# Twelve spare slots for the next expert's weights in a mixture-of-experts loop, emptied into the ring by GpSimd copies

## The reference, cut to what matters

```python
def moe_ffn(h, w_router, b_router, w_gate, b_gate, w_up, b_up, w_down, b_down):
    ...
    top_vals, top_idx = lax.top_k(logits, TOP_K)
    top_gates = jax.nn.softmax(top_vals, axis=-1)
    ...
    def expert_block(args):
        xb, e = args
        gate = xb @ w_gate[e] + b_gate[e]
        up = xb @ w_up[e] + b_up[e]
        gate = jnp.minimum(gate, SWIGLU_LIMIT)
        up = jnp.clip(up, -SWIGLU_LIMIT, SWIGLU_LIMIT)
        glu = gate * jax.nn.sigmoid(SWIGLU_ALPHA * gate)
        return (glu * (up + 1.0)) @ w_down[e] + b_down[e]
```

## Time and profile before

| | us |
|---|---|
| median of 3 runs | 2936.56 |
| lowest and highest run | 2932.51, 2937.8 |
| the profiled execution, its own time | 2935.62 |
| its span, first to last instruction | 2933.9 |
| TensorE busy in the span | 2772.3 |
| VectorE busy | 1529.7 |
| ScalarE busy | 956.0 |
| GpSimd busy | 116.1 |

### The profile page before, as it was taken

The page is one execution under the profiler, slowest core; times in us unless marked ns, Lnnn a source line. Parts: engine busy times, 40 slices in busy tenths (PEclk is TensorE's granted clock), DMA queues, the critical chain, the costliest instruction groups (busy, mean ns, idle before and its releaser), DMA issues.

```text
span 2933.9 us, 38779 instructions
## 1 busy us (share of the span) xinstructions
PE 2772.3 (94%) x12664; PEld 1659.5 (57%) x12664; DVE 1529.7 (52%) x3078; ACT 956.0 (33%) x1805; POOL 116.1 (4%) x171
## 2 busy tenths in 40 slices
PE   7899999999999999999999989999998999998997
PEld 5676678888778667888877753332322332322332
DVE  5984778875673554334385544343333343332435
ACT  4734342222563434222333322322222232222231
POOL 0000000000000003000020000000000000000002
PEclk9999999999999999999999979999999999999999
DMA  8271246864323035342323079689899789899897
GB/s 268 72 215 42 89 130 185 238 185 130 94 86 86 15 86 171 95 119 79 97 73 106 1 279 409 267 349 410 319 410 409 297 322 410 319 410 410 326 407 285
DMA packets 398912, 638.18 MB, mean 218 GB/s; under 512 B 34576, under 2 KB 284560, under 8 KB 398816
## 3 DMA queue, kind: packets, MB, share of 16 engines
q1 hardware_dynamic: 381024, 590.80, 55.9%
q0 software_dynamic: 9376, 31.14, 3.1%
q10 hardware_dynamic: 8416, 14.95, 1.4%
HBM read 610.79 MB, written 26.02 MB: 217 GB/s over the span
## 4 chain that ended last, share of the span: by engine, by line
PE 73%; DMA 9%; SPq 5%; DVE 5%; ACT 4%; issue 2%; POOL 0%; ACTq 0%; DVEq 0%; POOLq 0%
PE bank L2620 24%; PE bank L196 14%; PE bank L198 14%; PE bank L197 13%; DMA ring<-w_down 6%; SPq L2430 4%; DMA ring<-w_gate 2%; PE bank L1084 1%; PE bank L1125 1%; PE bank L1085 1%; DVE WLO L167 1%; ACT WHI L157 1%; PE bank L2614 1%; PE bank L1118 0%; ACT la L411 0%
## 5 line engine op out<-in xcount | busy, mean ns | idle before, releaser
L2620 PE MATMUL bank<-ring,xT 128*64 128x512 f32 x3200 | 728.8, 597 | 24.6 <-DMA ring<-w_up 12.7
L196 PE MATMUL bank<-HH,WHI 128*128 128x512 f32 x1344 | 540.2, 402 | 34.5 <-DVE WLO L167 17.3
L197 PE MATMUL bank<-HL,WHI 128*128 128x512 f32 x1344 | 529.9, 394 | 0.0
L198 PE MATMUL bank<-HH,WLO 128*128 128x512 f32 x1344 | 529.6, 394 | 0.0
L2620 PEld LDWEIGHTS bank<-ring,xT 128*64 128x64 f32 x3200 | 220.3, 137 | 496.8 <-issue 363.0
L2620 PE MATMUL bank<-ring,hT 128*64 128x512 f32 x1600 | 372.5, 601 | 26.1 <-DMA ring<-w_down 26.1
L167 DVE TENSOR_TENSOR WLO<-RAW,WHI 128x2048 fp32r<-128x2048 f32 (+1 forms) x132 | 281.6, 2134 | 105.7 <-ACT WHI L157 105.5
L196 PEld LDWEIGHTS bank<-HH,WHI 128*128 128x128 f32 x1344 | 256.8, 191 | 98.4 <-DVE WLO L167 23.0
L157 ACT ACTIVATE WHI<-RAW 128x2048 fp32r<-128x2048 f32 (+1 forms) x132 | 234.6, 1777 | 165.0 <-PE bank L198 129.7
L197 PEld LDWEIGHTS bank<-HL,WHI 128*128 128x128 f32 x1344 | 256.7, 191 | 55.5 <-issue 2.9
L198 PEld LDWEIGHTS bank<-HH,WLO 128*128 128x128 f32 x1344 | 256.3, 191 | 54.6
(11 more groups left out here) (462 smaller groups left out, 2776.7 us busy)
## 6 DMA issues: line engine op xcount, KB each, us to landing
ring<-w_gate SPq DMA_DIRECT2D x256, 512.0 KB, 9.4
ring<-w_up SPq DMA_DIRECT2D x256, 512.0 KB, 15.5
ring<-w_down SPq DMA_DIRECT2D x256, 512.0 KB, 15.1
RAW<-w_ffn_in SPq DMA_DIRECT2D x88, 512.0 KB, 5.2
RAW<-w_ada SPq DMA_DIRECT2D x40, 1024.0 KB, 5.2
RAW<-w_in SPq DMA_DIRECT2D x37, 1024.0 KB, 5.4
RAW<-w_ffn_out SPq DMA_DIRECT2D x32, 704.0 KB, 4.7
expert_results<-ysb ACTq DMA_DIRECT2D x98, 128.0 KB, 5.5
```

Of the source, the lines that this page charges most:

```text
L196: pe.matmul(out, lhi, rhi, start=start, stop=False)
L197: pe.matmul(out, lhi, rlo, start=False, stop=False)
L198: return pe.matmul(out, llo, rhi, start=False, stop=stop)
L2620: ins = pe.matmul(out[halves(h), :], xT[:, k % 4, halves(k // 4)], m["ring"][:, c, h * 512:(h + 1) * 512], start=False, stop=k == KD - 1)
```

## The change

The tile `ring` becomes `slots`, 39 slots from 40 KB on. Slots 15 to 38 are the old ring, at its old place; slots 0 to 11 are new and hold the first twelve slices (the 8 gate slices and the first 4 up slices) of the expert that comes next. n2x moves from 46 KB to 38 KB.

- **SyncE**: a new section `staged(i)` stands at the head of each pass. If block i is the first of its expert and another expert follows, it loads slices 0 to 11 of the *following* expert into the spare slots, each as soon as GpSimd has made the copy of that slot for block i. Slices 0 to 11 are no longer loaded into the ring; `loads` starts at slot 12. In the routing SyncE also waits for `nexts`, `stored` and `picked`.
- **GpSimd**: from pass 1 on, twelve copies per block, slot by slot. Each waits until TensorE has used ring slot c for the block before and until the staged slice has landed (a count from a register), and writes ring slot c. Its source is the spare slot c if the block begins an expert, and ring slot c itself if not. The index copy and the gather come after the twelve copies.
- **TensorE**: waits for the copy (`taken`) instead of the load for slots 0 to 11.
- **The routing**: VectorE computes four more small tables (next expert, whether a block begins an expert, the count to wait for, the source slot) and TensorE two more small products for them, and one for the place of the preceding expert. n2x is written after tokcol. TensorE waits for the first gather itself; before, GpSimd waited and passed it on.

```diff
@@ route_program, SyncE
         sp.wait_ge(*sg.event("bei"))
+        for c in range(STAGED):
+            sp.wait_ge(*sg.event("nexts")).then_inc(mo.sem[f"mo_st{c}"], 16)
+        sp.wait_ge(*sg.event("stored"))
+        sp.wait_ge(*sg.event("picked"))
         return
@@ route_program, VectorE
+        v.tensor_scalar(m["behind"][:], b[5][0:32, 208:240], pos, 1.0, ALU.subtract, ALU.is_equal)
         v.tensor_scalar(grid, b[5][0:32, 208:240], pos, None, ALU.is_gt).then_inc(*sg.inc("ro_dve", also=[("ahead", None)]))
...
+        v.tensor_tensor(m["prevc"][:], keyc, b[5][0:32, 201:202], ALU.subtract)
...
+        v.wait_ge(*sg.event("cmp"))
+        v.tensor_scalar(m["cmp3"][:], m["i48"][0:32, :], m["prevc"][:], None, ALU.is_ge).then_inc(*sg.inc("ro_dve", also=[("cmp3", None)]))
...
         v.memset(m["seld"][:], 0.0)
+        v.wait_ge(*sg.event("tokens"))
+        v.tensor_scalar(m["tokcol"][:], b[7][:, 0:NB + 1], vec[:, V2_HALF:V2_HALF + 1], None, ALU.add).then_inc(*sg.inc("ro_dve", also=[("tokcol", None)]))
         for k in range(KD):
             v.tensor_scalar(m["n2x"][:, k % 4, k // 4 * BLK:(k // 4 + 1) * BLK], one[:, 0:BLK], vec[:, V2_N2 + k:V2_N2 + k + 1], None, ALU.mult)
-        v.wait_ge(*sg.event("tokens"))
-        v.tensor_scalar(m["tokcol"][:], b[7][:, 0:NB + 1], vec[:, V2_HALF:V2_HALF + 1], None, ALU.add).then_inc(*sg.inc("ro_dve", also=[("tokcol", None)]))
+        nextf, heldf = m["nextf"][:, 1:NB], m["heldf"][:, 0:NB]
+        v.wait_ge(*sg.event("nextp"))
+        v.tensor_copy(m["nextf"][:, 0:NB], b[6][0:1, 336:336 + NB]).then_inc(*sg.inc("ro_step"))
+        v.wait_ge(*sg.last("ro_step"))
+        v.tensor_copy(m["nxt"][:, 0:NB], m["nextf"][:, 0:NB])
+        v.memset(m["heldf"][:, 0:1], 1.0)
+        v.tensor_tensor(m["heldf"][:, 1:NB], nextf, m["nextf"][:, 0:NB - 1], ALU.not_equal).then_inc(*sg.inc("ro_step"))
+        v.wait_ge(*sg.last("ro_step"))
+        v.tensor_tensor_scan(m["ordf"][:, 0:NB], one[0:1, 0:NB], heldf, 0.0, ALU.mult, ALU.add).then_inc(*sg.inc("ro_step"))
+        v.wait_ge(*sg.last("ro_step"))
+        v.tensor_scalar(m["level"][:, 0:NB], m["ordf"][:, 0:NB], 16.0, None, ALU.mult)
+        v.tensor_scalar(m["from"][:, 0:NB], heldf, -float(RING_SLOT), float(RING_SLOT), ALU.mult, ALU.add)
+        v.tensor_tensor(heldf, heldf, m["nextf"][:, 0:NB], ALU.mult).then_inc(*sg.inc("ro_step"))
+        v.wait_ge(*sg.last("ro_step"))
+        v.tensor_scalar(m["turnover"][:, 0:NB], heldf, 1.0, None, ALU.min).then_inc(*sg.inc("ro_dve", also=[("nexts", None)]))
@@ route_program, TensorE and GpSimd
-        pe.wait_ge(*sg.event("x0"))
+        pe.wait_ge(mo.sem["mo_x"], 16)
...
-        pool.wait_ge(mo.sem["mo_x"], 16)
-        pool.nop().then_inc(*sg.inc("ro_pool", "x0", also=[("x0", None)]))
         pool.wait_ge(*sg.event("tx0"))
+        pool.wait_ge(*sg.event("nexts"))
+        pool.nop().then_inc(mo.sem["mo_taken"], mo.total("mo_taken"))
@@ moe_load, moe_sp
-def moe_load(sp, m, W, c, e):
+def moe_load(sp, m, W, c, e, place=RING_SLOT):
     w = W[f"w_{MOE_CHUNKS[c][0]}_2"][0][e].rearrange("(k p) n -> p k n", p=P)
-    return sp.dma_start(m["ring"][:, c, :], w[:, MOE_CHUNKS[c][1], :])
+    return sp.dma_start(m["slots"][:, place + c, :], w[:, MOE_CHUNKS[c][1], :])
...
+    def staged(i):
+
+        e = sp.value_load(m["nxt"][0:1, bass.ds(i, 1)], min_val=0, max_val=EXPERTS - 1)
+        turnover = sp.value_load(m["turnover"][0:1, bass.ds(i, 1)], min_val=0, max_val=1)
+        with sp.If(turnover == 1):
+            for c in range(STAGED):
+                sp.wait_ge(*sg.event("taken", c, loop=i, back=1))
+                moe_load(sp, m, W, c, e, 0).then_inc(sg.sem[f"mo_st{c}"], 16)
+
     with sp.Fori(0, count) as i:
-        loads(i, "bei", "fresh", range(0, DOWN_FROM))
+        staged(i)
+        loads(i, "bei", "fresh", range(STAGED, DOWN_FROM))
         loads(i, "bed", "freshd", range(DOWN_FROM, MOE_SLOTS))
@@ moe_pe
+    def ready(c, i, first):
+
+        if c >= STAGED:
+            pe.wait_ge(*sg.event("raw", c, loop=i))
+        elif first:
+            pe.wait_ge(sg.sem[f"mo_first{c // KD}"], 16 * KD)
+        else:
+            pe.wait_ge(*sg.event("taken", c, loop=i, back=1))
@@ moe_pool
+    gather(0).then_inc(sg.sem["mo_x"], 16)
+    pool.sem_clear(sg.sem["mo_idx"])
+    with pool.Fori(1, count) as i:
+        first = pool.value_load(m["from"][0:1, bass.ds(i, 1)], min_val=0, max_val=RING_SLOT)
+        level = pool.value_load(m["level"][0:1, bass.ds(i, 1)], min_val=16, max_val=16 * EXPERTS)
+        for c in range(STAGED):
+            pool.wait_ge(*sg.event("used", c, loop=i, back=1))
+            pool.wait_ge(sg.sem[f"mo_st{c}"], level)
+            pool.tensor_copy(m["slots"][:, RING_SLOT + c, :], taken_from(m, c, first)).then_inc(*sg.inc("mo_taken", also=[("taken", c)]))
+        gather(i).then_inc(*sg.inc("mo_x", also=[("gathered", None)], n=16))
         pool.sem_clear(sg.sem["mo_idx"])
@@ moe_tensors
-    at("ring", 100, [P, MOE_SLOTS, D])
+    at("slots", 40, [P, RING_SLOT + MOE_SLOTS, D])
```

More of the change, by code:

```diff
@@ L2134 @@
 UP_FROM, DOWN_FROM = KD, 2 * KD
-MOE_SIGNALS = "mo_gain mo_end mo_last mo_first0 mo_first1 mo_first2 mo_act mo_dve mo_pe mo_down mo_idx mo_x mo_y " + " ".join(f"mo_raw{c}" for c in range(MOE_SLOTS))
-MOE_SEEDED = ("mo_act", "mo_dve", "mo_pe", "mo_down", "mo_x", "mo_y")
+STAGED, RING_SLOT = 12, 15
+MOE_SIGNALS = "mo_gain mo_end mo_last mo_first0 mo_first1 mo_first2 mo_act mo_dve mo_pe mo_down mo_taken mo_idx mo_x mo_y " + " ".join(f"mo_raw{c}" for c in range(STAGED, MOE_SLOTS)) + "".join(f" mo_st{c}" for c in range(STAGED))
+MOE_SEEDED = ("mo_act", "mo_dve", "mo_pe", "mo_down", "mo_x", "mo_y", "mo_taken")
 class LoopSignals(Signals):
@@ L2393, in route_program @@
         pe.matmul(b[5][0:32, 200:201], m["grid"][:], m["nbf"][:], start=True, stop=True)
+        pe.matmul(b[5][0:32, 201:202], m["behind"][:], m["nbf"][:], start=True, stop=True)
         pe.matmul(b[6][:, 192:224], m["nbf"][:].broadcast_to([32, P]), m["grid"][:], start=True, stop=True).then_inc(*sg.inc("ro_pe", also=[("firsts", None)]))
@@ L2397, in route_program @@
         pe.matmul(b[5][:, 256:256 + NB + 1], m["ord"][:, 66:67].broadcast_to([32, P]), m["cmp2"][:], start=False, stop=True).then_inc(*sg.inc("ro_pe", also=[("bep", None)]))
+        pe.wait_ge(*sg.event("cmp3"))
+        pe.matmul(b[6][0:1, 336:336 + NB + 1], m["ord"][:, 65:66], m["cmp3"][:], start=True, stop=False)
+        pe.matmul(b[6][0:1, 336:336 + NB + 1], m["ord"][:, 66:67], m["cmp"][:], start=False, stop=True).then_inc(*sg.inc("ro_pe", also=[("nextp", None)]))
         pe.wait_ge(*sg.event("ohb"))
@@ L2487, in by_features, with taken_from @@
     return tile[32 * q:32 * q + 32, :].rearrange("p (k h u c) -> p k h u c", k=4, h=2, u=2)[:, :, h, u, :]
+def taken_from(m, c, first):
+    return m["slots"][:, bass.ds(first + c, 1), :].rearrange("p o n -> p (o n)")
 def moe_act(act, sg, fi, m, b, W, count):
@@ L2619, in products @@
         for h in range(2):
-            ins = pe.matmul(out[halves(h), :], xT[:, k % 4, halves(k // 4)], m["ring"][:, c, h * 512:(h + 1) * 512], start=False, stop=k == KD - 1)
+            ins = pe.matmul(out[halves(h), :], xT[:, k % 4, halves(k // 4)], m["slots"][:, RING_SLOT + c, h * 512:(h + 1) * 512], start=False, stop=k == KD - 1)
         return ins
+    def ready(c, i, first):
[5 more added lines that the diff above has]
+            pe.wait_ge(*sg.event("taken", c, loop=i, back=1))
     def gate_up(i, first=False):
@@ L2632, in gate_up @@
         for c in range(UP_FROM):
-            pe.wait_ge(*sg.event("raw", c, loop=i))
+            ready(c, i, first)
             products(c, b[0], m["xT"]).then_inc(*done(("used", c), *[("g", None)] * (c == UP_FROM - 1)))
@@ L2683, in moe_pool, with gather @@
 def moe_pool(pool, sg, fi, m, W, count):
-    with pool.Fori(0, count) as i:
+    def gather(i):
         pool.wait_ge(*sg.event("xr", loop=i, back=1))
@@ L2717, in moe_tensors @@
     at("ohb", 40, [P, 16, NB + 1])
-    at("n2x", 46, [P, NT, P])
+    at("n2x", 38, [P, NT, P])
     at("h2t", 48, [P, NT, D])
@@ L2726, in moe_tensors @@
                                ("bef", [P, NB + 1]), ("bei", [1, NB + 1], I32), ("fresh", [1, NB + 1], I32), ("i48", [P, NB + 1]), ("rs4", [P, 4]),
-                               ("bed", [1, NB + 1], I32), ("freshd", [1, NB + 1], I32), ("tokcol", [P, NB + 1], U32), ("idx", [P, 1], U32),
+                               ("bed", [1, NB + 1], I32), ("freshd", [1, NB + 1], I32), ("nxt", [1, NB + 1], I32), ("from", [1, NB + 1], I32), ("turnover", [1, NB + 1], I32), ("tokcol", [P, NB + 1], U32), ("idx", [P, 1], U32),
                                ("fs", [P, 4])))):
@@ L2745, in moe_tensors @@
     at("cmp", 197.375, [32, NB + 1])
+    at("level", 197.6875, [1, NB + 1], I32)
     at("pb", 64, [P, TOP, P])
@@ L2752, in moe_tensors @@
     at("pos", 45.25, [32, 1])
+    at("prevc", 45.375, [32, 1])
+    at("behind", 45.5, [32, EXPERTS])
+    at("cmp3", 45.625, [32, NB + 1])
```

(3 more changed lines are left out.)

10 lines of the change are left out of this document (5 added, 5 removed).

## The result

The changed kernel takes 2945.25 us (median of 13 runs, 2939.71 to 2951.00) against 2937.80 (13 runs, 2932.51 to 2940.61) for the kernel before: a ratio of 1.0026, 95% interval 1.0019 to 1.0034. It is 7.45 us slower. The profiled execution took 2945.94 us, its span 2944.3.

A forecast was written before the change was run, and what follows sets the result against it. TensorE's beat of 21.26 us a block bounds it, plus 94.9 us of stalls ended by down-slot transfers. Terms 14.9 - 7.6 + 1.2 = +8.5 us on the median 2936.6 give 2945 us; range 2933 to 2968.

The forecast's parts named there:

- The order of the loads: SyncE's loads: as many slots before each stall-ending down slot as before, so stalls only move to up and down slots; 0.
- S1 to S4: Full DMA stretches at blocks 9 to 14, 17 to 24, 28 to 33 and 36 to 43; stalls priced unchanged, 0.
- S0: Full DMA stretch, blocks 1 to 5: first filling of spare slots costs +16.3 us, less 1.4 for earlier start: +14.9.
- S5: Last full DMA stretch, blocks 46 to 48: nothing staged behind the last expert, so its 7.6 us stall goes: -7.6.
- Starts of S1 to S4: Where these stretches begin, a transfer waits for GpSimd's copy, not TensorE's last use: +0.3 us each, +1.2 together.
- Copies: GpSimd's twelve copies per block: 1.05 us each, step 1.11, sum 17.3 with other work, below the beat of 21.26.
- The other price: GpSimd copy by the skill's 1.8 cycles an element: 1.54 us, sum 23.2, over TensorE's beat; set aside for the CAST row.
- Side by side by luck of phase: Within a block, GpSimd's copies end before VectorE's two-input work; one slipped copy delays xT 1.1 us, within 5.8 slack.
- GpSimd becomes the bound: Rival, chance 0.13: expert-loop copy step of 1.66 us exceeds the beat on 39 beats, +105 us, above about 3050.

The follow-up runs named there:

- The split order: Changed kernel, staged loads last where only the block before began an expert, eight first and four last where only the next begins one: 2916.40 us.
- the two kernels that differ in it: Changed kernel with copies only for blocks that begin an expert: 2948.80 us; the same with the first filling of spare slots left out: 2932.07 us.
- the short copies: Changed kernel with GpSimd copies of 64 columns instead of 1024: 2943.09 us, 1.0026 to the kernel before.

## Why the prediction was right

- **The order of the loads (price 0 in S1 to S4): right, and shown.** Gate stalls became stalls for up slots (the waits for down slots didn't grow, as the prediction had them do), block 18 to 22 takes 115.0 us against 114.5, and the stretches end as they did. The split order, with the same spare slots and the same copies, takes 29 us off the changed kernel (2945.25 to 2916.40).
- **S0, predicted +14.9, measured 14.1** by the gc rows, and 13.3 for the filling by the two kernels that differ in it, 1.11 us a slot where 1.36 was priced (less 1.4 for the earlier start). The terms: three operations before ohb gave 0.5; the transposes of tk ended at 1745.45, less the 2.7 of this execution 1742.8 (predicted 1743.0); the first staged load was issued at 1748.45, less 2.7 is 1745.8 (predicted near 1746).

```profile
1743.51 1.94 PE L2436 MATMUL bank<-K,tk 128*128 128x128 f32 x8 [8.16 <-DVE tk L2380]
```

```profile
1748.45 4.88 SPq L2458 DMA_DIRECT2D slots<-w_gate  x8
```

  One piece held by luck. The first gate products were to start about 3 us later; they do (5.0, of which 2.7 are this execution's), but without those 2.7 they end no later, since they take 7.06 us in place of 9.52. Before, the granted clock was 0.50 from 1742 to 1745 us, at their start; after, it is 1.00 from 1748 on. As transfers end S0's stalls, nothing hung on it.

```profile
1742.39 9.52 PE L2620 MATMUL bank<-ring,xT 128*64 128x512 f32 x32
```

```profile
1747.43 7.06 PE L2663 MATMUL bank<-slots,xT 128*64 128x512 f32 x32
```

- **S5, predicted -7.6, measured -7.6** (block 47's shift 18.2, block 49's 10.6), and no stall at blocks 48 and 49.
- **Starts of S1 to S4, predicted +1.2, measured +1.5** (block 10's shift 16.7, block 47's 18.2). The sum is near, its parts aren't: -0.1, +0.5, -0.1 and +1.2 for S1 to S4, where +0.3 each was priced, so the nearness is in part luck. That the copy lies in the path is shown by the short copies (0.7 to 0.9 a stretch); why S4 pays most is open. Predicted sum +8.5, measured 7.45 on the medians.
- **Copies: right in kind, a little dear.** Predicted 1.05 and a step of 1.11; measured 1.039, and twelve in 11.85, a step of 0.99:

```profile
2149.30 4.73 DVE L2603 SCALAR_TENSOR_TENSOR hh<-th,uc 32x128 f32<-32x128 f32 x16
2155.46 11.85 POOL L2753 COPY slots<-slots 128x1024 f32 x12 [7.25 <-PE bank L2663]
```

  The other price, which the Trainium skill gives (GPSIMD Engine Reference, Performance versus the Vector engine: 1.8 cycles an element at best), would by the prediction's estimate have made 1.54 us; the row has 1.04. Against the limit of 1.59 that dearer price would have stood at the very edge of the rival, just under it for a step of 1.54 and just over it with the hop of 0.06 that the prediction adds.
- **"Side by side by luck of phase" was the weak sentence, though it held.** The prediction priced a slipped copy at 1.1 us of xT's slack. What it missed is hh, at the other end of the block: between hh's end at 2154.03 and the first copy at 2155.46 lie 1.4 us. At block 0 the two do meet in the changed kernel (hh takes 9.35 us), and the long stall of block 2 parts them. The kernel with the filling left out shows what happens where they stay together: 2.54 us on every block, for 19 blocks. A rival for it was missing; by an estimate from these rows it would have cost up to 99 us over the 39 quiet beats.
- **The rival "GpSimd becomes the bound"** was real, but further off and cheaper than priced: by estimate it begins at a step of 1.59, and a step of 1.75 costs 72 us, where +105 was priced for 1.66.

## What to carry to other kernels

A deeper buffer takes a stall away only if its loads don't stand in front of a transfer that is due sooner: put the refill behind what is due sooner, and ahead of every wait that loads nothing. Count the slots between the start of a full stretch and each landing that ends a stall; in this kernel, where neither that count nor the start of the stretch changed, the time didn't either. With the twelve slots and the copies kept, the order alone was worth 29 us, four times what the change lost.

## What was unexpected

Two engines that hold each other up can lock into a second stable beat: hh of 13.82 us in place of 4.73 and blocks of 23.80 us in place of 21.26, with the same instructions in the same order, started by a different first block and ended by the next long stall for transfers. TensorE is 93% busy there and 94% in the changed kernel, so TensorE's busy share doesn't show it; VectorE's 1705.9 us against 1537.1 does, and hh in the grouped view: 851 ns a piece from 1780 to 2160 us, where the changed kernel has 283.
